# Start addresses of the split inputs, shifted against the split weights in a kernel of four rooms

## What is computed

```python
def peer_ffn(h, w_q, sub_keys, u, v):
    ...
    def chunk(args):
        hc, ic, gc = args
        a = jnp.einsum('cd,ced->ce', hc, u[ic])
        a = jax.nn.gelu(a, approximate=False) * gc.astype(hc.dtype)
        return jnp.einsum('ce,ced->cd', a, v[ic])
...
def conv_glu(hn, w_in, conv_w, conv_b, w_out):
    u, gate_in = jnp.split(hn @ w_in, 2, axis=-1)
    c = (conv_w[0] * shift_right(gate_in, 2) + conv_w[1] * shift_right(gate_in, 1)
         + conv_w[2] * gate_in + conv_b)
    return (jax.nn.gelu(c, approximate=False) * u) @ w_out
```

## Time and profile before

| | us |
|---|---|
| median of two runs | 2019.29 |
| the two runs | 2016.72, 2021.86 |
| the profiled execution | 2021.86 |
| its span, first to last instruction | 2021.6 |
| TensorE busy with matmuls (PE) | 1877.1 |
| TensorE busy with weight loads (PEld) | 1800.7 |
| VectorE busy (DVE) | 1456.5 |
| ScalarE busy (ACT) | 1242.6 |

### The profile page before, as it was taken

How to read it: one execution, slowest core, us unless ns; L and a number is a source line. 1 busy time by engine, 2 the same in 40 slices (tenths; PEclk the granted TensorE clock), 3 DMA queues, 4 the chain that set the end, 5 groups by cost and what they waited for, 6 DMA issues and landing times. The chain is left out here.

```text
span 2021.6 us, 45016 instructions
## 1 busy us (share of the span) xinstructions
PE 1877.1 (93%) x16518; PEld 1800.7 (89%) x16518; DVE 1456.5 (72%) x3046; ACT 1242.6 (61%) x2420; POOL 0.2 (0%) x4
## 2 busy tenths in 40 slices
PE   8998988999999999999999989687999977999997
PEld 8887888999999976899999989587999976899996
DVE  7667667688985479766666667776888678578857
ACT  5454655777776789655555556733665555666555
POOL 0000000000000000000000000000000000000000
PEclk9999999999999999999999999798999989999998
DMA  6533344466655620266666646101665644166562
GB/s 208 158 97 105 118 143 136 132 194 193 179 186 175 186 84 0 84 194 190 196 191 193 193 139 199 52 3 56 184 196 173 192 126 136 34 190 189 176 198 76
DMA packets 102084, 296.06 MB, mean 146 GB/s; under 512 B 9539, under 2 KB 32454, under 8 KB 101830
## 3 DMA queue, kind: packets, MB, share of 16 engines
q1 hardware_dynamic: 101958, 294.35, 47.0%
HBM read 293.26 MB, written 1.05 MB: 146 GB/s over the span
## 5 line engine op out<-in xcount | busy, mean ns | idle before, releaser
L459 DVE TENSOR_TENSOR w_low<-ring,w_high 128x512 fp32r<-128x512 f32 x1102 | 743.2, 685 | 357.1 <-ACT w_high L453 349.2
L503 PE MATMUL bank<-a_high,w_high 128*128 128x256 f32 x3228 | 921.2, 285 | 74.3 <-DVE w_low L459 39.1
L504 PE MATMUL bank<-a_low,w_high 128*128 128x256 f32 x3228 | 907.5, 281 | 0.0
L505 PE MATMUL bank<-a_high,w_low 128*128 128x256 f32 x3228 | 907.4, 281 | 0.0
L453 ACT ACTIVATE w_high<-ring 128x512 fp32r<-128x512 f32 x1102 | 671.4, 624 | 375.3 <-PE bank L505 372.8
L503 PEld LDWEIGHTS bank<-a_high,w_high 128*128 128x128 f32 x3228 | 620.0, 192 | 90.0 <-DVE w_low L459 39.7
L504 PEld LDWEIGHTS bank<-a_low,w_high 128*128 128x128 f32 x3228 | 616.3, 191 | 0.4
L505 PEld LDWEIGHTS bank<-a_high,w_low 128*128 128x128 f32 x3228 | 616.7, 191 | 0.0
L503 PE MATMUL bank<-s_high,w_high 128*128 128x256 f32 x1024 | 283.5, 277 | 2.0 <-DVE s_low L2446 2.0
L504 PE MATMUL bank<-s_low,w_high 128*128 128x256 f32 x1024 | 283.3, 277 | 0.0
L505 PE MATMUL bank<-s_high,w_low 128*128 128x256 f32 x1024 | 283.3, 277 | 0.0
(11 more groups left out here) (368 smaller groups left out, 1867.8 us busy)
## 6 DMA issues: line engine op xcount, KB each, us to landing
ring<-in_stream SPq DMA_DIRECT2D x273, 512.0 KB, 3.7
ring<-in_peer_u SPq DMA_DIRECT2D x128, 512.0 KB, 3.6
ring<-in_peer_v SPq DMA_DIRECT2D x128, 512.0 KB, 3.5
ring<-in_stream SPq DMA_DIRECT2D x32, 256.0 KB, 3.3
ring<-in_stream SPq DMA_DIRECT2D x12, 192.0 KB, 2.7
x<-in_x SPq DMA_DIRECT2D x4, 256.0 KB, 6.3
arena<-in_mem SPq DMA_DIRECT2D x1, 1024.0 KB, 11.0
out<-x SPq DMA_DIRECT2D x4, 256.0 KB, 2.6
```

The source lines that it names most:

```text
L459: self.nc.vector.tensor_tensor(self.cut(h, self.w_low), self.raw(h), self.cut(h, self.w_high.bitcast(F32)), ALU.subtract)\
L503: self.nc.tensor.matmul(to, lh, rh, start=start, stop=False, **more)
L504: self.nc.tensor.matmul(to, lh, rl, start=False, stop=False, **more)
L505: return self.nc.tensor.matmul(to, ll, rh, start=False, stop=stop, **more)
```

## The change

`room` gets a number `lift` of floats by which its arena is made longer. The pair behind it begins so much later; in the expert layer `hot` does too, and a tile of 16 floats, `s_lift`, stands ahead of `s_high`. No instruction touches the added bytes. The lifts are 8 floats (32 bytes) for the first mixer, 24 (96 bytes) for the expert layer with 16 more (64 bytes) for `s_high` and `s_low`, 0 for the hybrid and 120 (480 bytes) for the last room.

```diff
-    def room(self, floats, chunks=0):
-
+    def room(self, floats, chunks=0, lift=0):
 
         self.rooms += 1
-        with self.nc.sbuf_tensor(f"arena{self.rooms}", [P, floats], F32) as self.arena:
+        with self.nc.sbuf_tensor(f"arena{self.rooms}", [P, floats + lift], F32) as self.arena:
             self.scratch = self.arena[:, floats - 2 * T:floats].rearrange("p (c t) -> p c t", c=2)
...
     def peer(self):
 
-        with self.room(N_KEYS * T):
+        with self.room(N_KEYS * T, 0, 24):
             with self.pairs(DC):
                 self.peer_scores()
 
             with self.nc.sbuf_tensor("hot", [P, 2, 4, 4, P], F32) as hot:
                 self.expert_weights(hot)
-            with self.nc.sbuf_tensor("s_high", [P, SIDES, T], F32R) as s_high, \
+            with self.nc.sbuf_tensor("s_lift", [P, 16], F32), \
+                    self.nc.sbuf_tensor("s_high", [P, SIDES, T], F32R) as s_high, \
                     self.nc.sbuf_tensor("s_low", [P, SIDES, T], F32R) as s_low:
                 self.expert_sum(s_high, s_low)
...
-        with k.room(86 * T, 2 * DC):
+        with k.room(86 * T, 2 * DC, 8):
             k.first_mixer()
         k.peer()
-        with k.room(HYBRID_ROOM, DC + 3):
+        with k.room(HYBRID_ROOM, DC + 3, 0):
             out = k.hybrid()
-        with k.room(70 * T, DC + FC + 2):
+        with k.room(70 * T, DC + FC + 2, 120):
```

## The result

| | before | after |
|---|---|---|
| first measurement, median (runs), us | 2019.29 (2016.72, 2021.86) | 2060.16 (2059.98, 2060.35) |
| later, beside the experiments, us | 35 runs, 2018.85 to 2043.81 | 2060.83, 2064.59 |
| span of the profiled execution, us | 2021.6 | 2058.2 |

The ratio of after to before is 1.0196, with a 95% interval of 1.0157 to 1.0236; measured again beside the kernel before it was 1.0181 (1.0116 to 1.0246). Both intervals lie clear of 1, so the change makes the kernel slower; they also hold 1.02, so whether by less or more than 2% is not settled. The 37 executions of the kernel before that this study holds have a median of 2027.3 us, so its first two were lucky ones, and against that median the loss is 33 us, 1.6%. All ratios here leave out an execution of more than 1.5% above the fastest of its kernel; there is one, of 2051.4 us, in the first experiment.

A forecast was written before the change was run, and what follows sets the result against it. TensorE was taken to bound the kernel, busy 1877.1 of 2021.6 us. Long slow stretches at the fast pace (17.3 us) and short runs (0.7) gave 18 us off 2021.9, so 2004 us, range 1982 to 2038.

The forecast's parts named there:

- That TensorE bounds the kernel and a change of pace passes nearly one to one: Whole kernel: TensorE busy 1877.1 of 2021.6 us, no other engine near, so matmul pace passes nearly one to one into time.
- That nothing else is touched: All engines: same instructions, waits and DMAs in the same order, and input splits writing at other addresses; cost 0.
- That there are two paces which a restart chooses, by the meeting of streamed and loaded operand: Helper's three products: 113.3 or 117.8 ns per matmul, settled after TensorE stands still and held until it does again.
- the second restart: TensorE's 1.99 us wait at 1554.74 us, read as the change from the slow pace to 113 ns.
- The slow pattern goes, 18 us: Helper's products: 458 us of slow stretches at the fast pace save 17.3 us, short runs 0.7.
- the middle case: Whole kernel: a stream of only fast stretches at 113.3 ns, 2004 us; slow pattern gone or nearly had 0.50.
- The upper bound, 2057: Helper's products: slow pattern everywhere, 8450 more matmuls at 4.45 ns, 35 us after waits absorb some, 2057 us.
- The lower bound, 111.4 ns: Helper's products at the best weight-load pace seen for "hot": 24 us more saved, 1980 us.
- the rival "much faster": Helper's products: without meetings of the two reads the pace goes to 111.4 ns, 1980 us; chance 0.09.
- The rival "slower": Peer_v loop: odd distances choose the slow pattern or need one fetch more; 13.7 us more, 2036 us; chance 0.19.
- The rival "no change": Helper's products: both patterns stay with the same odds at each restart, 2019 us; chance 0.22.
- The base: Starting time of the kernel before, 2021.9 us; its two runs may differ by one long stretch worth 4 us.

The follow-up runs named there:

- the first experiment: Split weights, arenas and split inputs all begin 32 bytes later than in the kernel before, distance still 448; 2034.1 us, ratio 1.0000.
- the five profiles counted above: Kernel before; all tiles 32 bytes later (2034.1 us); distance 192 (2030.2); second and third matmul exchanged (2032.3); only s_high and s_low at 480 (2040.9).

## Why the prediction was wrong

- **That TensorE bounds the kernel and a change of pace passes nearly one to one**: right. 40 us of slower matmuls became 36.6 us of span.
- **That nothing else is touched**: right. VectorE's and ScalarE's busy time grew by 1.5 and 2.8 us. TensorE's wait for weights did not grow.
- **That there are two paces which a restart chooses, by the meeting of streamed and loaded operand**: right in the main. The paces follow the distance of the two and not the tile's own start (all tiles moved), and the same kernel draws otherwise in another execution. That it is a meeting of two reads fits this, but no run shows the reads themselves, nor why the sets repeat after 256 bytes. The two paces are those of 448 and 192; five more stand at other distances. And the second restart was read a little wrongly. The pace does not change at the wait before 1554.74 us but at 1551.10, at a halt so short that the timeline marks no idle time:

```profile
1550.94 0.28 PE L505 MATMUL bank<-a_high,w_low 128*128 128x256 f32 x1
1551.10 0.39 PE L503 MATMUL bank<-a_high,w_high 128*128 128x256 f32 x1
1551.33 0.28 PE L504 MATMUL bank<-a_low,w_high 128*128 128x256 f32 x1
```

From 1551.33 to 1552.47 us ten matmuls take 1.14 us, 114 ns each. Between halts the pace does hold: of the 196 stretches of 40 matmuls and more without one, in the five profiles counted above, none ends at another pace than it begins with.
- **The slow pattern goes, 18 us**: this is the step that failed. It rested on the supposition that operands are fetched in pieces of 64 bytes, so that a shift by 32 would let the fetches pass each other. The sets repeat after 256 bytes and not after 64. The odd distances do not free the stream of its slow pattern, they take the good one away: among the multiples of 32 tried, 113.3 ns exists only at 448 and 192, and seldom at 64. I had written "nothing in the rows points to odd as worse" and took the middle case because it asked for nothing new; but the row for the odd distances did not exist, and with no row on either side the middle had no claim over the ends. Some 8500 of the 12,756 matmuls already ran in the best pattern known, so there was more to lose than to win, as the rival's "for" said.
- **The upper bound, 2057**: sized too low. It took 117.8 ns as the worst. The worst is 120.0, as in the loop over peer_v, where I had priced the loss at 13.7 us and it was 20.5. Everything at 120.0 is 2077 us, as distance 0 shows.
- **The lower bound, 111.4 ns, and the rival "much faster"**: nothing between 111 and 113 ns appeared at any distance. 113.3 is the best that these matmuls reached. The 109.2 ns of the Trainium skill's page "TensorE: Matmul & The Clock Gate", section "Back-to-back issue gap", which it gives as the gap of an isolated matmul and not of a stream with weight loads, were not seen either.
- **The rival "slower"**: this is the case that came, nearest to its first mechanism (the odd distances choose a slow pattern, though at 120.0, 118.3 and other paces and not at the known 117.8) and not by its second (an extra fetch), which the run with all tiles moved excludes. Its place, the loop over peer_v, was right, and it had 0.19.
- **The rival "no change" and the rule behind it**: the rule of the Trainium skill's page "SBUF — State Buffer", section "Who interferes with whom", that TensorE's two read ports are independent, would have the distance not matter. Measured, it matters by up to 120.0 - 113.3 = 6.7 ns per matmul, 6%. The measurement decides; that the two reads hold each other up is the likely reading, argued and not shown.
- **The base**: I took 2021.9 as typical and the difference of the two runs as one long stretch. The kernel before has a median near 2027. So some 8 of the 41 us between the first medians are luck of the base.

## What to carry to other kernels

Where TensorE loads a block for every matmul of 256 fp32r columns, as here, the start of the streamed tile against the loaded one, modulo 256 bytes, is a parameter of the kernel and worth 6% of the matmuls' pace. Measure it over all eight multiples of 32 before a layout is settled, and read the pace from a stretch's length over its count, since the mean duration hides it. A kernel whose pace is drawn at restarts needs many executions before two of its versions can be compared, and where no row shows the new condition, a forecast has to give both ends their due.

## What was not expected of the hardware

- The paces are few and sharp: 113.3, 116.7, 117.3, 117.8, 118.3, 118.7 and 120.0 ns for the same instruction at a granted clock of 1.00, with both input tiles at one distance. Which of them occur goes with the distance modulo 256 bytes, in all eight multiples of 32; one can hold for a stretch of 3070 matmuls.
- The best pace needs the high and the low tile at the good distance together: with only the low ones moved, 117.6 to 119.3 ns.
- A restart at distance 448 or 192 ends at 113.3 ns in nearly two of three cases (288 of 449 in four profiles), though over 40% of the cases are short runs of 9 to 11 matmuls. A halt that adds some 0.12 us to two starts is enough for a new draw.
